# Expert rows stored by token and rank, idle lanes skipped, biases put into the PSUM banks by ACT

## The reference, cut to what matters

```
logits = xf @ w_router + b_router
top_v, top_e = top_k(logits, 4);  gates = softmax(top_v)
# for each expert e and each token that chose it:
gu   = xe @ w_gu[e] + b_gu[e]                       # 1024 -> 2048, gate and up interleaved
gate = min(gu[..., 0::2], 7);  up = clip(gu[..., 1::2], -7, 7)
act  = (up + 1) * (gate * sigmoid(1.702 * gate))
y    = act @ w_dn[e] + b_dn[e]                      # 1024 -> 1024
out[token] += y * gate_of_token_and_expert
x = rms_norm(x + out, final_norm_g)
```

## Time and profile before

| What | Value |
|---|---|
| median of 3 runs | 1615.03 us (1613.72 to 1615.38) |
| profiled execution, whole | 1609.29 us |
| its span, first to last instruction | 1607.5 us |
| mean granted clock of PE | 0.956 |
| PE's matmuls for the lane tables end | 359.9 us |
| first expert matmul starts | 381.67 us |
| DVE's last copy of turned activations ends | 1566.7 us |
| last y copy of ACT ends | 1580.9 us |

### The profile page before, as it was taken

The page is one execution under the profiler, slowest core; times in us unless marked ns, Lnnn a source line. Parts: engine busy times, 40 slices in busy tenths (PEclk is TensorE's granted clock), DMA queues, the critical chain, the costliest instruction groups (busy, mean ns, idle before and its releaser), DMA issues.

```text
span 1607.5 us, 20866 instructions
## 1 busy us (share of the span) xinstructions
PE 1479.8 (92%) x7011; PEld 1227.5 (76%) x7011; DVE 1293.3 (80%) x1228; ACT 1020.8 (64%) x902; POOL 236.1 (15%) x148
## 2 busy tenths in 40 slices
PE   5999889755899999999999999999999999999983
PEld 5777667644788888888888888888888888888872
DVE  5227753474899999999999999999999999999991
ACT  5335433313677777777777777777777777777771
POOL 0000000000011122211111222111112211111120
PEclk9999999657999999999999999999999999999996
DMA  9311030604899999999999999999999999999974
GB/s 349 105 54 53 27 131 13 223 24 180 304 347 377 385 370 372 382 388 381 388 381 379 375 372 381 385 388 381 387 376 378 375 374 384 385 386 386 377 263 131
DMA packets 97674, 486.12 MB, mean 302 GB/s; under 512 B 8217, under 2 KB 8242, under 8 KB 63794
## 3 DMA queue, kind: packets, MB, share of 16 engines
q1 hardware_dynamic: 87250, 448.05, 71.3%
q0 software_dynamic: 10400, 37.75, 9.0%
HBM read 461.65 MB, written 24.12 MB: 302 GB/s over the span
## 4 chain that ended last, share of the span: by engine, by line
PE 87%; issue 5%; DVE 5%; DMA 2%; ACT 1%; SPq 0%; DVEq 0%; POOLq 0%; POOL 0%; ACTq 0%
PE gu_bank L1031 17%; PE gu_bank L1032 17%; PE gu_bank L1033 17%; PE turn_bank L1031 8%; PE turn_bank L1032 8%; PE turn_bank L1033 8%; PE gu_bank L1226 2%; PE bank L1233 2%; PE bank L1240 2%; PE bank L1031 1%; PE bank L1165 1%; PE bank L1033 1%; PE bank L1032 1%; DVE w_lo L697 1%; PE turn_bank L1148 1%
## 5 line engine op out<-in xcount | busy, mean ns | idle before, releaser
L697 DVE TENSOR_TENSOR w_lo<-raw,w_hi 128x2048 fp32r<-128x2048 f32 x412 | 934.9, 2289 | 129.1 <-ACT w_hi L493 125.0
L493 ACT ACTIVATE w_hi<-raw 128x2048 fp32r<-128x2048 f32 x412 | 789.5, 1920 | 238.9 <-PE gu_bank L1033 184.1
L1031 PE MATMUL gu_bank<-w_hi,turned 128*128 128x512 f32 (+1 forms) x1104 | 432.3, 392 | 7.0 <-DVE turned L950 7.0
L1032 PE MATMUL gu_bank<-w_lo,turned 128*128 128x512 f32 (+1 forms) x1104 | 429.3, 389 | 0.0
L1033 PE MATMUL gu_bank<-w_hi,turned 128*128 128x512 f32 (+1 forms) x1104 | 429.1, 389 | 0.0
L1031 PEld LDWEIGHTS gu_bank<-w_hi,turned 128*128 128x128 f32 x1104 | 208.2, 189 | 49.2 <-issue 5.8
L1033 PEld LDWEIGHTS gu_bank<-w_hi,turned 128*128 128x128 f32 x1104 | 208.1, 188 | 42.8
L1032 PEld LDWEIGHTS gu_bank<-w_lo,turned 128*128 128x128 f32 x1104 | 208.3, 189 | 41.5
L1031 PE MATMUL turn_bank<-w_hi,turned 128*128 128x512 f32 (+1 forms) x544 | 211.5, 389 | 2.0 <-DVE turned L955 2.0
L1032 PE MATMUL turn_bank<-w_lo,turned 128*128 128x512 f32 (+1 forms) x544 | 211.0, 388 | 0.0
L1033 PE MATMUL turn_bank<-w_hi,turned 128*128 128x512 f32 (+1 forms) x544 | 210.3, 387 | 0.0
(11 more groups left out here) (206 smaller groups left out, 1354.5 us busy)
## 6 DMA issues: line engine op xcount, KB each, us to landing
raw<-in_w_gate_up_dram SPq DMA_DIRECT2D x264, 1024.0 KB, 8.8
raw<-in_w_down_dram SPq DMA_DIRECT2D x132, 1024.0 KB, 10.9
raw<-in_w_in_dram SPq DMA_DIRECT2D x10, 1024.0 KB, 8.3
raw<-in_w_out_dram SPq DMA_DIRECT2D x4, 1024.0 KB, 5.2
raw<-in_w_mem_kv_dram SPq DMA_DIRECT2D x2, 1024.0 KB, 8.7
arena<-in_x_dram SPq DMA_DIRECT2D x1, 2048.0 KB, 14.4
arena<-in_position_tables_dram SPq DMA_DIRECT2D x1, 2048.0 KB, 19.5
arena<-in_x_dram SPq DMA_DIRECT2D x2, 1024.0 KB, 5.5
```

Source lines behind the costliest of these rows:

```text
L493: a.activation(w_hi[:, slot, :], raw_ap, ACT.Copy).then_inc(hi_ready, 1)
L697: v.tensor_tensor(w_lo[:, slot, :], raw_ap, w_hi[:, slot, :].bitcast(F32), ALU.subtract).then_inc(lo_ready, 1)
L1031: pe.matmul(bank, a[0], b[0], start=first, stop=False)
L1032: pe.matmul(bank, a[0], b[1], start=False, stop=False)
```

## The change

- Every expert row goes to a DRAM row of its own, `expert_rows[4 * token + rank]`, rank being the position of the expert among the token's four by number. The scatter stores without adding. Idle lanes get an index beyond the bounds in both the gather and the scatter, and are skipped.
- `x1` stays in SBUF and isn't written to DRAM. After the loop the rows of the four ranks are read back (ranks 0 and 1 during the last block, rank 2 behind the last but one scatter, rank 3 behind the last) and DVE adds them; the inverse root is taken for two pairs of tiles.
- The bias table, the selections and the bias matmuls go. For each block SP loads one row with the expert's gate/up bias and the previous expert's down bias; POOL copies it to 128 partitions (`spread`); ACT copies it into the PSUM banks (`seed_gu`, two instructions, and `seed_y`, one), and PE's matmuls all accumulate onto it. Six matmuls ahead of the loop write each bank once. ACT takes the sigmoid into `act` directly.
- Around the loop: DVE's bias table and POOL's load of `final_norm_g` ahead of the first gather are gone (the latter moves to SP at the end), SP loads the first bias rows before it goes on with the weights, and waits each iteration for `bias_ready`.

```diff
+            def biases(e_gu, e_y):
+                sp.dma_start(bias_row[:, 0:2 * FF], b_gate_up[0][e_gu, :]).then_inc(bias_in, 16)
+                sp.dma_start(bias_row[:, 2 * FF:3 * FF], b_down[0][e_y, :]).then_inc(bias_in, 16)
             sp.wait_ge(tab_ready, 1)
+            biases(slice(0, 1), slice(0, 1))
             loops = sp.value_load(loops_i[0:1, :], min_val=E - 1, max_val=MAX_LOOPS)
             with sp.Fori(1, loops + 1) as b:
                 before, e = (sp.value_load(exp_i[0:1, bass.ds(b + i, 1)], min_val=0, max_val=E - 1)
                              for i in (-1, 0))
+                sp.wait_ge(bias_ready, b)
+                biases(bass.ds(e, 1), bass.ds(before, 1))
...
-            pool.dma_start(g_final, final_norm_g.unsqueeze(0).to_broadcast([P, D])).then_inc(gf_in, 16)
...
+            def spread(n_in):
+                pool.wait_ge(bias_in, n_in)
+                pool.sem_inc(spread_go, 1)
+                pool.partition_broadcast(bias_rows, bias_row).then_inc(bias_ready, 1)
             gather(slice(0, 1), 1)
+            spread(32)
             pool.wait_ge(xtp_done, 1)
             gather(slice(1, 2), 2)
+            pool.wait_ge(gu_seeded, 1)
+            spread(64)
...
-                pool.indirect_dma_start(sum_dram, bass.IndirectOffsetOnAxis(idx_scatter, 0),
-                                        y_row, None, compute_op=ALU.add).then_inc(y_sent, 16)
+                pool.indirect_dma_start(y_dram, bass.IndirectOffsetOnAxis(idx_scatter, 0), y_row, None,
+                                        bounds_check=TOPK * S - 1, oob_is_err=False).then_inc(y_sent, 16)
             with pool.Fori(1, loops + 1) as b:
                 pool.wait_ge(xtp_done, b + 1)
                 gather(bass.ds(b + 1, 1), b * 2 + 1)
+                pool.wait_ge(gu_seeded, b + 1)
+                pool.wait_ge(y_seeded, b)
+                spread(b * 32 + 64)
                 scatter(b - 1, b * 2 + 2)
...
+            def seed_gu(n, read=None):
+                a.wait_ge(bias_ready, n)
+                if read is not None:
+                    a.wait_ge(sig_ready, read)
+                banks, rows = (z.rearrange("p (i two) -> p two i", two=2) for z in (gu_psum[:, :], bias_rows[:, 0:2 * FF]))
+                a.activation(banks[:, 0, :], rows[:, 0, :], ACT.Copy)
+                a.activation(banks[:, 1, :], rows[:, 1, :], ACT.Copy, bias=1.0).then_inc(gu_seeded, 1)
+            def seed_y(n, read=None):
+                a.wait_ge(bias_ready, n)
+                if read is not None:
+                    a.wait_ge(y_free, read)
+                a.activation(turn_psum[:, :], bias_rows[:, 2 * FF:3 * FF], ACT.Copy).then_inc(y_seeded, 1)
...
-                sigmoid(b + 1)
+                sigmoid(b + 1, b)
                 turn_x(0, b + 2)
                 turn_x(1, b + 2)
+                seed_gu(b + 2, b + 1)
                 for i in range(12, 16):
                     hi_m(GU + i, b)
                 y_out(b * 12 + (16 + GU), bass.ds(b - 1, 1), b * 16)
+                seed_y(b + 2, b + 1)
...
-                v.wait_ge(gu_done, n)
+                v.wait_ge(half_used, used)
...
+            for r in range(TOPK):
+                for t in range(NT):
...
+                    v.tensor_tensor(x1[t], x1[t], rows, ALU.add).then_inc(fin_sum, 1)
...
-                pe.wait_ge(sig_ready, b)
+                pe.wait_ge(gu_seeded, b + 1)
...
-                gu_bias(b + 1)
                 pe.wait_ge(alo_ready, b * 2)
                 turn_rows(b * 16 + 32)
-                y_bias(b - 1)
+                pe.wait_ge(y_seeded, b)
```

More of the change, by code:

```diff
@@ L208, in hymba_layer @@
         idx_scatter = F[:, 15001:15002].bitcast(I32)
-        bias_in = F[0:2 * E, 0:3 * FF]
+        bias_rows = F[:, 8192:8192 + 3 * FF]
+        bias_row = F[0:1, 11264:11264 + 3 * FF]
         h_row = F[:, 4096:5120]
[L213 to L216, removed]
+        y_row = F[:, 5120:6144]
+        up_t, act = F[:, 6144:7168], F[:, 7168:8192]
+        g_final = F[:, 8192:9216]
+        back = raw[:, 0:NT, :]
+        third = [raw[:, 4 + t // 2, t % 2 * D:(t % 2 + 1) * D] for t in range(NT)]
+        fourth = [F[:, 4096 + t * D:4096 + (t + 1) * D] for t in range(NT)]
         hx, lx = (R[:, i * D:(i + 1) * D].rearrange("p (k s) -> p k s", k=KT) for i in (0, 1))
         ha, la = (R[:, i * D:(i + 1) * D].rearrange("p (k s) -> p k s", k=KT) for i in (2, 3))
-        bias = R[:, 4 * D:7 * D]
-        pick = R[:, 7 * D:7 * D + P]
-        pick_y = R[:, 7 * D + P:7 * D + 2 * P]
         gains_turned, gains_ready = sem("gains_turned"), sem("gains_ready")
@@ L404, in _ @@
             gate_up(0, 5, 5)
[L405 to L408, removed]
+            for t in (0, 2, 3):
                 sp.wait_ge(normed, 6 + t + 1)
@@ L988, in _ @@
                 lo_m(i)
-            clamp(1)
-            choose(pick, pick_ready, slice(1, 2))
-            choose(pick_y, pick_y_ready, slice(0, 1))
+            clamp(1, 16 + GU)
             lo_m(GU + 2)
@@ L1217, in gate_up @@
                 for c in range(4):
-                    ins = three(psum[c], (hx[:, k, :], lx[:, k, :]), w_part(slot, c * 512, (c + 1) * 512),
-                                first=k == 0)
+                    ins = three_onto(psum[c], (hx[:, k, :], lx[:, k, :]), w_part(slot, c * 512, (c + 1) * 512))
                 ins.then_inc(half_used, 1)
-            def gu_bias(n_pick):
-                pe.wait_ge(pick_ready, n_pick)
-                for c in range(4):
-                    ins = pe.matmul(psum[c], pick, bias[:, c * 512:(c + 1) * 512], start=False, stop=True)
-                ins.then_inc(gu_done, 1)
             def turn_rows(n_h):
@@ L1242, in turn_acts @@
                 ins.then_inc(atp_done, 1)
-            def y_bias(b):
-                pe.wait_ge(y_free, b + 1)
-                pe.wait_ge(pick_y_ready, b + 1)
-                for c in range(2):
-                    ins = pe.matmul(psum[4 + c][:, :], pick_y, bias[:, 2 * FF + c * 512:2 * FF + (c + 1) * 512],
-                                    start=True, stop=False)
-                ins.then_inc(ybias_done, 1)
             def down(j, i, b):
@@ L1258, in down @@
                         at0 = kk * D + c * 512
-                        ins = three(psum[4 + c], (ha[:, k, :], la[:, k, :]),
-                                    w_part(slot, at0, at0 + 512), last=k == KT - 1)
+                        ins = three_onto(psum[4 + c], (ha[:, k, :], la[:, k, :]), w_part(slot, at0, at0 + 512))
                 ins.then_inc(half_used, 1)
+            pe.wait_ge(tab_ready, 1)
+            pe.wait_ge(hi_ready, 17)
+            for c in range(6):
+                ins = pe.matmul(psum[c], act_hi[:, 0, 0:P], w_hi[:, 0, 0:512], start=True, stop=True)
+            ins.then_inc(banks_open, 1)
             turn_rows(16)
+            pe.wait_ge(gu_seeded, 1)
             pe.wait_ge(xlo_ready, 1)
```

163 lines of the change are left out of this document (91 added, 72 removed).

## The result

The changed kernel takes 1687.28 us, the median of 4 runs (1684.54 to 1696.52), against 1614.38 (1612.60 to 1615.38, 4 runs) of the kernel before beside it: a ratio of 1.0464, 95% interval 1.0445 to 1.0483. It is slower, and by more than rival (a) gave. The profiled execution took 1688.41, span 1686.3, mean granted clock 0.938.

A forecast was written before the change was run, and what follows sets the result against it. PE was taken to bound the loop, DVE having 2.5 us to spare. -31 - 10 - 0.4 + 1 - 1 + 2.3 = -39 us from 1609.29 gave 1570 profiled, 1576 as median; range 1560 to 1669.

The forecast's parts named there:

- rival (a): POOL's read holds up DVE's low splits before the clamp: 37.8 us a block, +62 instead of -31, 1669 us; chance 0.23.
- Part 2: In the loop, POOL's broadcast of the bias rows runs beside DVE's clamp, G + 1.5 to 4.9, and costs 0 us.
- G: Time mark in each block: the end of PE's last gate/up half, from which the prediction counted its steps.
- The size of the copy: POOL's copy of 3072 bias values to 128 partitions: 3.35 us chosen, 1.75 below and 6.7 above.
- rival (b): In the loop, the broadcast ends late without port conflict, delaying the seeds: 38.6 us a block, 1694 us, or 36.6, 1632; chance 0.10.
- Part 1: In the loop, bias matmuls leave PE, which then waits 0.3 to 0.4 us: block 34.8 us, gain 1.0, 31 times.
- the hand-over: From the loop's first block to the second: loses 0.4 us, counted as -0.4 in the sum.
- Part 3: Loop transfers, idle lanes skipped, need 34.3 us a block at 381 GB/s, under 34.8: no gain of their own.
- Part 4: Before the loop: tables ready 5.2 us sooner, first gate/up matmul near 372: -10 us, bounds -6 and -10.
- Part 5: The end: +1 for the last block's later split, -1 for the plain-store scatter, +2.3 for two square-root chains.

The follow-up runs named there:

- e3_late: Changed kernel, with POOL's copy in the loop also waiting until PE has used the last gate/up half: 1585.07 us, ratio 0.9815.
- e9_before_late: Kernel before, with an added unused POOL copy of 3072 values a block, released behind the last gate/up half: 1616.36 us, ratio 1.0021.
- e1_tiny: Changed kernel, with POOL copying only 1 of the 3072 bias values in the loop, loads, waits and seeds kept: 1584.99 us, ratio 0.9818.
- e4_fill: Changed kernel, with 12 useless matmuls a block added in PE's wait ahead of half 0: 1669.64 us, ratio 1.0345.
- e6_late_hi: Changed kernel, with POOL's copy behind the last gate/up half and half 0's high split ahead of ACT's two seeds: 1562.92 us, ratio 0.9689.
- e8_rows_alone: Kernel before, with every part of the change but the biases (row per token and rank, idle lanes skipped, x1 kept): 1613.07 us, ratio 1.0001.
- e7_before_copy: Kernel before, with an added unused POOL copy of 3072 values a block, released after the seventh of eight gate/up halves: 1715.46 us, ratio 1.0651.
- e10_one_root: Changed kernel with late copy and high split ahead of seeds, plus one inverse root over four tiles instead of two: 1565.32 us, ratio 0.9710.

## Why the prediction was wrong

It gave 1576 us and 0.66 to a gain. The profiled spans differ from its sum by 117.8 us: +78.8 where -39 was worked out. The steps, one by one:

**Part 2 failed, at one step: when the bias rows land.** The argument had three links. That the copy and DVE's splits exclude each other is right. That POOL can copy beside the clamp without loss is right, as e3_late and e9_before_late show. That the copy would be there at that time is wrong: I took the median of the weights' landing (9.5 us, of 1 MB transfers) for two rows of 8 and 4 KB. The rows were issued at 1000.23 and 1000.71, 8.8 us ahead of G as worked out, and the copy began at 1007.83, 7.1 us behind the second, and at 1044.96 in the next block, whose rows were issued at 1038.03 and 1038.51, 10.3 ahead of its G. PE's last gate/up half ends at 1009.00 and 1048.35, where the windows above were cut. So the copies begin 1.2 and 3.4 us ahead of G, in DVE's back-to-back splits, and within the bounds that the step itself had named (G - 4 to G + 3). The early end of those bounds is rival (a). I used the bounds for the size of the copy and took the middle for its place, though the place had the larger price and nothing in the program fixed it: the copy was released by a transfer. Price of this step: e1_tiny's 32 blocks take 1123.1 us, e4_fill's 1208.4, so 85.3 us; against e3_late, which has the whole copy at the right place (1124.6), 83.8.
The Trainium skill (SBUF — State Buffer, "Who interferes with whom") has the second of the two wait for the whole of the first. The rows agree both ways round, to about 0.3 us: split 4.93 us behind the copy, copy 5.40 us behind the split.

**The size of the copy** was 3.30 us where I chose 3.35, by luck: the number came from a DVE instruction, and no POOL row stood behind it. 0.26, 1.80 and 3.30 us for 1, 1536 and 3072 values are 1.0 ns a value.

**Rival (a)** had place, mechanism and block length right: 37.8 forecast, 37.76 in e4_fill. Its sign, a low split of 4 us and more, came. Its condition, rows landed by G - 1, fits too: the copy at G - 0.6 (1434.94) did no harm, the one at G - 1.2 did. Its chance of 0.23 was too low, and its reason against (no stretched split in the trace before) was no evidence, as no long POOL read stood beside one there.

**Missing term: the clock.** 18.7 us (1227.1 less 1208.4). A wait of 2.9 us in each block was followed in many of them by about 3 us of matmuls at 1.2 GHz. This is why the result lies above even rival (a), and above the stated range, whose upper end was (a) although rival (b) went to 1694.

**Part 1** held. Seeds of 1.02 us (1.0 taken), low split at G + 12.15 in e3_late (12.1), a wait of 0.4. A block came to 35.16 (31 of them) instead of 34.8, a gain of 0.66 instead of 1.0: the wait of 0.40 costs 0.66, and even without a wait a block is 34.53. The first stretch came out 0.6 us longer than before (33.04 against 32.40) where the hand-over was to make it 0.4 shorter. Over 32 blocks 1123.1 against 1142.8 - 31.4 = 1111.4: 11.7 us too little. 85.3 + 18.7 + 11.7 = 115.7, which is the whole error in the loop (84.3 + 31.4); that the three add up is no proof, since they are differences along one chain of runs.

**Part 3** held: transfers were no bound at 34.5 us a block (e6_late_hi), and skipping lanes gave nothing by itself (e8_rows_alone).

**Part 4** held apart from what lies ahead of it. From tables ready to the first gate/up matmul: 365.71 to 375.86, 10.15 us, where 10.3 was worked out; before it was 14.8. But the tables were ready only 1.2 us sooner instead of 5.2, because the whole of DVE's work ahead of them came 4.1 us later (354.83 against 350.77 for the same instruction, which the change doesn't touch). Between 200 and 250 us the granted clock was 0.83 and then 0.89 in this execution, 0.91 and 1.00 in the kernel before. It isn't the change: in all 13 profiles the same instruction starts at 350.65 to 352.12 where the clock is 0.91 and 1.00 (the kernel before, e6_late_hi, e7_before_copy, e9_before_late, e10_one_root), and at 353.47 to 355.65 where it is 0.83 and 0.89 (the other eight), e6_late_hi having the code of the kernel after there. It also fits most of the 5.7 us by which the profiled execution lay below its median.

**Part 5**: scatter to landing 3.23 us instead of 6.08, then from the last landing (1671.04) to the end 15.3 instead of 12.0. The gain and the loss nearly cancel, +1.0 from the last clamp on, and e8_rows_alone is level with the kernel before.

## What to carry to other kernels

Where two engines share something that only one can have, don't ask whether a new instruction fits into a gap, but what releases it. If a transfer does, its place is a range, and each place in it has its own price; tie it to the event that opens the gap, as one added wait did here for 102 us. Once a wait has appeared on the engine that bounds the kernel, price it with its restart and with a possible fall of the clock, and look at the unit behind the one you freed before promising what a new order brings.

## What the runs showed of the hardware

- A copy of 3072 float32 values from one partition to 128 takes POOL 3.30 us alone and 1536 values 1.80 us. Beside a low split of DVE, one of the two stands still: 4.75 and 4.93 us for a split of 2.29 in the rows above, up to 5.40 for a copy of 3.30. Beside a clamp that reads PSUM neither loses (3.24 us for the copy, 1.22 for the clamp).
- POOL's issue of an indirect store stood still in 16 blocks, 10.66 us against 1.88, beside a run of splits without gaps; that the splits are the cause is not shown.
- A matmul wait that the profile shows as 0.40 us costs PE 0.66 us: 0.79 instead of 0.23 us from start to start across it, and 0.33 behind it.
- Behind waits of 2.84 to 3.00 us the granted clock was 0.50 for about 3 us in many blocks (1025.41 to 1028.40), in others not. 12 matmuls in the wait kept it at 1.00 and saved 18 us.
- 400 GB/s on one core, where the kernel before moved 381 at a share of 1.00: a full share was not the ceiling.
- The same attention code ran about 4 us longer in some executions than in others, at a clock of 0.83 and 0.89 instead of 0.91 and 1.00.
